# HGRN2 decay levels of a four-mixer decoder in 64 by 64 parts on four quarters of the array, with masked copies over all 128 partitions

## The reference

```python
f = lb + (1 - lb) * sigmoid(fl);  logf = log(f);  k = (1 - lb) * sigmoid(-fl)
def step(S, inp):                      # one chunk
    qb, kb, vb, gb = inp
    b = cumsum(gb, axis=2)
    decay = where(causal, exp(b_t - b_s), 0)
    attn = einsum('bhtd,bhtsd,bhsd->bhts', qb, decay, kb)
    o = einsum('bhts,bhsv->bhtv', attn, vb) + einsum('bhtd,bhdv->bhtv', qb * exp(b), S)
    S = S * exp(b_last) + einsum('bhsd,bhsv->bhdv', kb * exp(b_last - b), vb)
```

## Time and profile before

| what | value |
|---|---|
| median of 3 launches | 1959.87 us (1957.77 to 1960.52) |
| profiled execution, own time | 1956.64 us |
| its span, first to last instruction | 1954.8 us |
| mean granted TensorE clock | 0.997 of 2.4 GHz |
| TensorE busy | 1921.2 us (98%) |
| VectorE busy | 957.6 us (49%) |
| ScalarE busy | 783.0 us (40%) |
| GpSimd busy | 968.8 us (50%) |

### The profile page before, as it was taken

How to read it: one execution, slowest core, us unless ns; L and a number is a source line. 1 busy time by engine, 2 the same in 40 slices (tenths; PEclk the granted TensorE clock), 3 DMA queues, 4 the chain that set the end, 5 groups by cost and what they waited for, 6 DMA issues and landing times.

```text
span 1954.8 us, 31312 instructions
## 1 busy us (share of the span) xinstructions
PE 1921.2 (98%) x12436; PEld 1556.6 (80%) x12436; DVE 957.6 (49%) x1779; ACT 783.0 (40%) x1251; POOL 968.8 (50%) x1195
## 2 busy tenths in 40 slices
PE   8999999999999999999999999999999999999997
PEld 7876867778779888888998777677777798888887
DVE  7928986313434423223587479862234353223144
ACT  6534365125536322223474344732355362222223
POOL 2435435325375555557634444261254845555573
PEclk9999999999999999999999999999999999999999
DMA  5222311112232143322313123111121412322332
GB/s 186 71 84 68 97 54 55 45 45 65 65 119 87 54 151 97 97 97 97 97 30 104 59 76 97 42 58 44 34 86 56 139 55 76 108 97 97 97 97 76
DMA packets 52839, 159.37 MB, mean 82 GB/s; under 512 B 5217, under 2 KB 17633, under 8 KB 52449
## 3 DMA queue, kind: packets, MB, share of 16 engines
q1 hardware_dynamic: 51552, 154.65, 24.6%
q10 hardware_dynamic: 1152, 2.86, 0.4%
HBM read 155.39 MB, written 2.10 MB: 81 GB/s over the span
## 4 chain that ended last, share of the span: by engine, by line
PE 83%; DVE 9%; ACT 3%; POOL 2%; issue 1%; DMA 0%; DVEq 0%; ACTq 0%; SPq 0%
PE bank L659 24%; PE bank L661 22%; PE bank L660 22%; POOL w_lo L1784 2%; PE bank L860 1%; DVE slab L2201 1%; PE bank L1039 1%; DVE col L2194 1%; PE bank L798 1%; PE bank L769 1%; PE bank L994 1%; PE bank L784 1%; PE bank L1051 1%; DVE slab L2116 1%; DVE tmp L1883 0%
## 5 line engine op out<-in xcount | busy, mean ns | idle before, releaser
L1784 POOL TENSOR_TENSOR w_lo<-w_raw,w_hi 128x256 fp32r<-128x256 f32 x1072 | 830.8, 808 | 954.0 <-ACT w_hi L1311 657.2
L659 PE MATMUL bank<-hn_hi,w_hi 128*128 128x512 f32 x1248 | 511.6, 410 | 1.2 <-DVE slab L1936 0.9
L661 PE MATMUL bank<-hn_hi,w_lo 128*128 128x512 f32 x1248 | 487.4, 391 | 0.0
L660 PE MATMUL bank<-hn_lo,w_hi 128*128 128x512 f32 x1248 | 487.0, 390 | 0.0
L1719 ACT ACTIVATE w_hi<-w_raw 128x1024 fp32r<-128x1024 f32 x120 | 127.3, 1061 | 405.0 <-DMA w_raw<-wrest 404.9
L659 PE MATMUL bank<-u_hi,w_hi 128*128 128x512 f32 (+1 forms) x800 | 287.1, 359 | 1.4 <-DVE u_lo L1947 1.1
L659 PEld LDWEIGHTS bank<-hn_hi,w_hi 128*128 128x128 f32 x1248 | 234.3, 188 | 66.6 <-issue 20.0
L660 PE MATMUL bank<-u_lo,w_hi 128*128 128x512 f32 (+1 forms) x800 | 284.2, 355 | 0.0
L661 PE MATMUL bank<-u_hi,w_lo 128*128 128x512 f32 (+1 forms) x800 | 284.1, 355 | 0.0
L661 PEld LDWEIGHTS bank<-hn_hi,w_lo 128*128 128x128 f32 x1248 | 234.3, 188 | 50.3
L660 PEld LDWEIGHTS bank<-hn_lo,w_hi 128*128 128x128 f32 x1248 | 234.8, 188 | 44.6 <-issue 3.4
(11 more groups left out here) (395 smaller groups left out, 2924.9 us busy)
## 6 DMA issues: line engine op xcount, KB each, us to landing
w_raw<-wrest SPq DMA_DIRECT2D x136, 512.0 KB, 3.5
w_raw<-wmerge SPq DMA_DIRECT2D x80, 512.0 KB, 3.5
w_raw<-wproj SPq DMA_DIRECT2D x52, 512.0 KB, 3.5
wx_raw<-wproj SPq DMA_DIRECT2D x4, 512.0 KB, 4.8
wy_raw<-wproj SPq DMA_DIRECT2D x4, 512.0 KB, 7.9
slab<-rope ACTq DMA_DIRECT2D x2, 1024.0 KB, 6.4
wx_raw<-wrest SPq DMA_DIRECT2D x4, 512.0 KB, 5.1
wy_raw<-wrest SPq DMA_DIRECT2D x4, 512.0 KB, 5.0
```

What stands on the lines that cost most here:

```text
L659: mm(o_, stat[0], mov[0], start=first, stop=False)
L660: mm(o_, stat[0], mov[1], start=False, stop=False)
L661: return mm(o_, stat[1], mov[0], start=False, stop=last)
L1784: ins = pool.tensor_tensor(wchunk(1, s_)[:, cs], wload(s_)[:, cs], wchunk(0, s_)[:, cs].bitcast(f32), SUB)
```

## The change

The scores of HGRN2's levels 1 to 6 are made in 64 by 64 parts. A chunk of 128 keys is cut into two halves (`r`); each half's keys (64 columns of the stationary operand) meet only the 32 query columns of the same half. With two sides and two halves there are four kinds of `mm`, one for each quarter of the array: `side` chooses the rows, `r` the columns and with them the partitions of the result. A level is 32 `mm`s of 64 by 64 by 32 in place of 16 of 64 by 128 by 64. Level 7, in which the two halves of a chunk meet, is 16 `mm`s of 64 by 64 by 64 whose results lie in partitions 0 to 63. Level 0 is 32 `mm`s of 64 by 64 by 128.

A level now fills two banks, one for each side, with all four chunks, and alternates between banks 4, 5 and 6, 7. VectorE takes each with one `copy_predicated` of 128 by 512, and level 7 with a plain copy of 64 by 512. TensorE waits at level 1 for all four copies of level 0, and from level 3 on for those of two levels before. `AT` is laid out by side. VectorE's four level 0 copies stand behind `norm_raw` and `norm_lo` of the tiles 5 to 7, where they stood ahead of `norm_raw(6)`. The counts of dense steps and the order of the weight splits are unchanged.

```diff
-        a_sc = signal("a_scores_ready", 8 * NT)
-        a_sc_used = signal("a_scores_taken", 8 * NT)
+        a_sc = signal("a_scores_ready", NT + 7 * 2)
+        a_sc_used = signal("a_scores_taken", NT + 7 * 2)
...
                     pe.wait_ge(*a_ops.at(L, lv + 1))
-                    for pair in (0, 2):
-                        if lv:
-                            pe.wait_ge(*a_sc_used.at(L, (lv - 1) * NT + pair + 2))
-                        for i in range(4):
-                            c, t = pair + i // 2, i % 2
-                            cs = slice(c * P, (c + 1) * P)
-                            for b in (pair, pair + 1):
-                                lo = (b % 2) * HD
+                    n, E = LEVELS[lv - 1], S((5, 18)[(lv - 1) % 2])
+                    if lv:
+                        pe.wait_ge(*a_sc_used.at(L, NT + 2 * max(0, lv - 2)))
+                    for i in range(2 * NT):
+                        c, t = i // 2, i % 2
+                        for side in range(2):
+                            hs, bank_ = slice(side * HD, (side + 1) * HD), ps[4 + (2 * (i // NT) if lv == 0 else lv % 2 * 2) + side]
+                            for r in range(1 if lv == 7 else 2):
+                                rs, ts_ = slice(r * HD, (r + 1) * HD), slice(c * P + r * HD, c * P + (r + 1) * HD)
                                 if lv == 0:
-                                    ins = mm(ps[4 + b][:, i * P:(i + 1) * P], k_[lo:lo + HD, t, cs], S(0)[lo:lo + HD, t, cs],
+                                    ins = mm(bank_[rs, i % NT * P:(i % NT + 1) * P], k_[hs, t, ts_], S(0)[hs, t, c * P:(c + 1) * P],
+                                             start=True, stop=True)
+                                elif lv < 7:
+                                    m = i * HD + r * HD // 2
+                                    ins = mm(packed(bank_[rs, m:m + HD // 2], n), E[hs, t, ts_], halves(E[hs, t, ts_], n, 1),
                                              start=True, stop=True)
                                 else:
-                                    n, E = LEVELS[lv - 1], S((5, 18)[(lv - 1) % 2])
-                                    ins = mm(packed(ps[4 + b][:, i * HD:(i + 1) * HD], n), E[lo:lo + HD, t, cs],
-                                             halves(E[lo:lo + HD, t, cs], n, 1), start=True, stop=True)
-                                if i == 3:
-                                    ins.then_inc(*a_sc.up())
+                                    ins = mm(bank_[rs, i * HD:(i + 1) * HD], E[hs, t, ts_], E[hs, t, c * P + HD:(c + 1) * P],
+                                             start=True, stop=True)
+                            if i == 2 * NT - 1 or lv == 0 and i == NT - 1:
+                                ins.then_inc(*a_sc.up())
...
                 norm_raw(5)
                 norm_lo(4)
-                for c in range(NT):
-                    dve.wait_ge(*a_sc.at(L, c + 1))
-                    tt(heads(AT[c]), heads(ps[4 + c][:, :]), over_heads(C("ident")), MUL).then_inc(*a_sc_used.up())
                 for m in (6, 7):
                     norm_raw(m)
                     norm_lo(m - 1)
                 norm_lo(KT - 1)
+                for half in range(2):
+                    for side in range(2):
+                        dve.wait_ge(*a_sc.at(L, 2 * half + side + 1))
+                        tt(AT[side][:, half * NT:(half + 1) * NT, :], heads(ps[4 + 2 * half + side][:, :]), over_heads(C("ident")), MUL)\
+                            .then_inc(*a_sc_used.up())
                 bc = b_.rearrange("p (b n) -> p b n", n=P)
                 for lv in range(1, 8):
                     if lv < 7:
                         decayed(lv)
-                    for c in range(NT):
-                        dve.wait_ge(*a_sc.at(L, lv * NT + c + 1))
+                    n_ = LEVELS[lv - 1]
+                    for side in range(2):
+                        dve.wait_ge(*a_sc.at(L, NT + 2 * (lv - 1) + side + 1))
                         carry_wait()
-                        n_ = LEVELS[lv - 1]
-                        dve.copy_predicated(halves(AT[c], n_, 1).rearrange("p (h b) n -> p h b n", h=H),
-                                            level_half(lv - 1, n_), packed(ps[4 + c][:, 0:256], n_)
-                                            .rearrange("p (h b) n -> p h b n", h=H)).then_inc(*a_sc_used.up())
+                        bank_ = ps[4 + lv % 2 * 2 + side]
+                        if lv == 7:
+                            dve.wait_ge(*a_sc_used.at(L, NT + 6 * 2))
+                            dve.tensor_copy(AT[side][0:HD, :, HD:P], packed(bank_[0:HD, :], HD)).then_inc(*a_sc_used.up())
+                        else:
+                            dve.copy_predicated(AT[side].rearrange("p e (b two n) -> p e b two n", two=2, n=n_)[:, :, :, 1, :],
+                                                level_half(lv - 1, n_, 2 * NT), packed(bank_[:, :], n_).rearrange("p (e b) n -> p e b n", e=2 * NT))\
+                                .then_inc(*a_sc_used.up())
```

More of the change, by code:

```diff
@@ L381, in packed, with level_half @@
             return ap.rearrange("p (b n) -> p b n", n=n)
-        def level_half(k, n):
+        def level_half(k, n, nh):
             v = halves(msk[:, k * P:(k + 1) * P], n, 1)
-            return v[:, None, :, :].to_broadcast([P, H, P // (2 * n), n])
+            return v[:, None, :, :].to_broadcast([P, nh, P // (2 * n), n])
         def level(k):
@@ L867, in _ @@
                     if c == 0:
-                        pe.wait_ge(*a_sc_used.at(L, 8 * NT))
+                        pe.wait_ge(*a_sc_used.at(L, NT + 7 * 2))
                     else:
@@ L874, in _ @@
                     dense(("a_keys", c + 1))
-                AT = [slab[:, 16 + c // 2, (c % 2) * T:(c % 2 + 1) * T] for c in range(NT)]
+                AT = [slab[:, 16 + side, :].rearrange("p (e n) -> p e n", n=P) for side in range(2)]
                 v_ = slab[:, 4, :].rearrange("p (c n) -> p c n", c=NT)
@@ L886, in _ @@
                             lo = (h % 2) * HD
-                            at_ = AT[2 * (c // 2) + h % 2][:, (c % 2 * 2 + t) * P:(c % 2 * 2 + t + 1) * P]
+                            at_ = AT[h % 2][:, 2 * c + t, :]
                             mm(ps[5][lo:lo + HD, t * P:(t + 1) * P], v_[:, c, h * HD:(h + 1) * HD], at_, start=True, stop=False)
```

## The result

| what | before | after |
|---|---|---|
| median, 20 executions each on one chip | 1958.24 us (1956.71 to 1960.80) | 1963.39 us (1958.18 to 1967.22) |
| ratio to the kernel before, 95% interval | | 1.0023 [1.0014, 1.0032] |
| profiled execution, own time | 1956.64 us | 1960.55 us |
| span | 1954.8 us | 1958.8 us |
| mean granted TensorE clock | 0.997 | 0.991 |

The forecast was 1960.5 us, range 1956 to 1965, with most of the chance on a change within 0.2%. The range holds the median, which lies a little above the likeliest case's own upper end of 1963; the loss by the ratio, 4.5 us (2.7 to 6.3), is 0.23%, just beyond that bound of 0.2%. The executions of after lie in two groups, ten at 1958.2 to 1961.1 us and ten at 1965.7 to 1967.2 (those of before at 1956.7 to 1958.3 and 1959.9 to 1960.8), so none lies near the median of 1963.39, and the upper group is beyond the range's end of 1965.

A forecast was written before the change was run, and what follows sets the result against it. TensorE's in-order list was taken to bound the kernel. Two layers of burst savings less the copies' delay (-3.6 us) plus the fallen clock (+4.2 us) gave +0.6 us on 1959.87 us: 1960.5 us, range 1956 to 1965.

The forecast's parts named there:

- likeliest case: Stall ahead of HGRN2's level 1 and a fallen clock behind it; 1958 to 1963 us, chance 0.60.
- Bursts of levels 1 to 6: TensorE's 64-instruction bursts take 1.07 us each, saving 1.07 us at level 1 and 0.86 at each of five more.
- Level 7: Its burst of 32 instructions on two quarters takes 1.05 us, saving 0.88; its later copies cost 0 to 0.2, taken as 0.
- The moved copies: Level 0 copies behind VectorE's normalization make TensorE begin level 1 4.45 us later, with everything queued behind it.
- Sum without the clock: Per layer, savings of 6.25 us less a delay of 4.45 us: net -1.8 us, -3.6 for two layers.
- The clock: TensorE's stall of some 5 us ahead of level 1 drops its clock; 2.1 us a layer, +4.2 for two.
- Later waits: After level 1, TensorE meets no new wait for copies of two levels before or for the weight split behind level 4.
- rival 3: No stall at level 1, because VectorE reaches the copies early enough; about -12 us, 1948 us, chance 0.05.
- The sum: Whole program: -3.6 us without the clock's loss and +4.2 us for it give +0.6 us, 1960.5 us.
- (1): The clock holds through the stall at level 1; -3.6 us, 1956.3 us, chance 0.16.
- (2: Quarters don't overlap as in RWKV7, bursts of levels 1 to 6 run at 33 ns an instruction; 1972.9 us, chance 0.08.
- Rival 4: Longer stall at level 1 or clock low longer: 1 us more and 2.6 of clock per layer; 1963.5 us, chance 0.11.

The follow-up runs named there:

- filled wait: The changed kernel with 20 unused matmuls on TensorE ahead of level 1's wait; 1955.11 us, ratio 0.9987 to the kernel before.
- copies back: The changed kernel with the four level 0 copies, in their new form, put back ahead of norm_raw(6); 1951.08 us, ratio 0.9967 to the kernel before.
- copies early: The changed kernel with the four level 0 copies put ahead of norm_raw(4); 1949.71 us, ratio 0.9960 to the kernel before.
- two quarters in turn: The kernel with the copies early, with the loop over side outermost so neighbouring products use two quarters; 1955.08 us, ratio 0.9988 to the kernel before.

## Why the prediction was right, point by point

The mechanism was right: faster bursts, a wait of 5.3 us put in front of them, a fallen clock behind it, each found at its place. That the median of 1963.39 came to lie in the range owes something to luck. The forecast of +0.6 us was added to 1959.87 us, a median of three; on the 1958.24 us of twenty it would have been 1958.8, and the loss by the ratio is 4.5 us (2.7 to 6.3), several times the 0.6. The points below say where the difference lies: some 1.4 us in two terms of the sum, the rest outside the changed stage.

- **Bursts of levels 1 to 6: 1.07 us.** Right: 1.06 to 1.07 us wherever the clock reads 1.00. The 25 ns that the Trainium skill gives (TensorE: Matmul & The Clock Gate, "Wait — 56ns, not 53.3ns?") did not hold for four quarters in turn, at 17 ns; two in turn at 28 ns come near it.
- **Level 7: 1.05 us.** 1.08 us (109.06 less the burst's start at 107.98). Its two copies start 0.22 us after the next dense matmul, and the first transposes (L876) come at 110.70, 1.64 us behind that matmul where they came 1.49 behind it: within the 0.2 us of the bound.
- **Level 0 priced at nothing.** It took 53.85 - 51.94 = 1.91 us, 0.07 less than before, and the wait at level 1 covered it.
- **The moved copies: 4.45 us.** Counted from the scan, level 1 starts at 65.13 - 42.74 = 22.39 us where it started at 61.35 - 43.58 = 17.77: 4.62 us later. The copies stood at 62.5 to 65.0, about as forecast (63.3 to 65.7), the kernel being some 0.8 us earlier at its entry.
- **Sum without the clock: -1.8 us a layer.** The filled wait measures -1.57, the first of the two terms that were a little off. There level 1 is 65.15 - 42.84 - 17.77 = 4.54 us late, so the bursts give back 6.1 us, of the 6.25 in the sum.
- **The clock: 2.1 us a layer.** In the first profile 2.53 and 1.60, mean 2.07, but that this mean meets the forecast is luck: over the six stalls of the three profiles the cost is 1.6 to 3.1 us, mean 2.6, at the upper of the bounds of 1.7 and 2.6. The term was mis-sized by some 0.5 us a layer. 1.2 GHz lasts 6.84 us in all of them, not 4, and how much of that falls on work and not on the idle time (3.5 to 6.7 us) differs from stall to stall.
- **Later waits: none.** Right for the kernel after. In the two kernels where the wait at level 1 was cut, waits for the weights' low parts, which this step had ruled out for the kernel after, appear: 0.9 us a layer with the copies back and 2.25 with the copies early. The gains add up with them: 6.1 us from the bursts, less 1.31 us of longer wait at level 1 (1.88 for 0.57) and 0.9 is 3.9; and 6.1 plus the whole 0.57, less 2.25, is 4.4 us. So rival 3 was mis-sized at 12 us; the better kernel gains 8.7 us in two layers and 0.4% in time.
- **The sum: +0.6 us.** In the stage itself +0.98 us in the first profile. Over the three profiles of each kernel the two layers of HGRN2 take 153.65 us against 152.17, +1.5 us (+2.0 without the one low stretch that before had there), and RWKV7's part takes 230.45 against 227.50, +2.9 us, in the stretches at half clock at the end of its chunks. The mean spans differ by 5.9 us; what is left, 1.5 us, is most of it the second profile's stretches in attention and its later entry. So the larger part of the loss lies where no step of the prediction looked: it expected the change to be felt in HGRN2 alone. Part of RWKV7's share is the chance of one execution, since the copies early showed none or many of these stretches; but after had 10 to 14 us of them in each profile and before 3.4 us. What makes them likelier in after was not found. The fallen clock in HGRN2, hundreds of us earlier, is not needed for it: the copies back and the filled wait had 10.2 and 6.8 us without it.
- **The rivals.** The clock did not hold (1), the quarters overlapped (2; the two quarters in turn show the price of 28 ns that it needed to be right), the stall came (3). Rival 4, a clock that stays low longer, comes nearest to the median with its 1963.5 us. Half of it was so: the stall was 5.3 us as forecast and no longer, but the clock cost more than the sum had, 2.6 us a layer as the rival said. The rest of its 3.6 us came by another place than it named.

## What to carry to other kernels

When a change shortens the work of the engine that sets the pace and delays one handover in front of it, price the two apart: here 6.1 us saved per layer was for the most part eaten by 4.5 us of waiting, and the fallen clock behind the wait took the rest and more. Put the copy that the pacing engine waits for as early as its input allows (4.4 us a layer here, against a loss with the copy last), and look at once for the next producer that is now too late. Small products in parts of the array gained most here when neighbouring instructions used all four quarters in turn (1.07 us a burst, against 1.79 with two in turn and 1.93 with the old form), so the loop order belongs to the estimate.

## What the runs showed that was not expected

- Order of the quarters: 17 ns an instruction, the start of the burst included, for four in turn, 28 ns for two that share their rows, 64 columns by 32.
- A masked copy of 512 elements whose blocks are 1 or 2 elements took 1.25 us (2.50 us for two at level 1), in the later levels 0.66 us (1.33 us for two).
- VectorE's 128 by 512 step from slab to slab took 0.68 us, and 1.22 us while GpSimd was splitting weights. A masked copy at level 3, which reads one operand from a bank, was not slowed: 1.33 us for two beside GpSimd's split with the copies early. The Trainium skill (GPSIMD Engine Reference, "Specifications") says that GpSimd and VectorE share their way to SBUF, with contention for VectorE's instructions with two SBUF inputs; these times agree.
- The clock fell in places without a long idle time: in attention with TensorE busy 2.00 of 2 us, and in HGRN2 some 2 us behind a wait of 0.58 us, while an idle time of 1.88 us (copies back, both layers) passed at 1.00. The same place falls in one execution and not in the next.
- A fallen clock costs by what of it lies behind the wait: 1.6 to 3.1 us for the same 6.84 us at 1.2 GHz.
